# Rounds of four HGRN heads and of two mLSTM heads: loops on the engines, or the same rounds written out

## What is computed

```python
mod = silu(c) @ ada_w + ada_b                       # 2048 x 12288: shifts, scales, gates
h = rms_norm(x) * (1.0 + sc1) + sh1
proj = h @ w_in                                     # 2048 x 18448
hq, hf, hi, hg, mq, mk, mv, mi, mf, mo, ga, gb = split(proj)
o_hg, S_new = hgrn2_chunked(q, kk, logf, vv, S0)    # 16 heads of 128 x 128
y_a = head_rms_norm(o_hg, hg_norm_w) * silu(hg)
h_ml, C_new, n_new, m_new = mlstm_chunked(...)      # 8 heads of 128 x 256
y_b = head_rms_norm(h_ml, ml_norm_w) * sigmoid(mo)
merged = sigmoid(ga) * y_a + sigmoid(gb) * y_b
x = x + g1 * (merged @ w_out)
h = rms_norm(x) * (1.0 + sc2) + sh2
up = h @ w_up                                       # then a convolution of width 3 and gelu
x = x + g2 * (y @ w_down)
y = rms_norm(x, final_norm_w)                       # outputs: y, and all the new states
```

## Time and profile before

| | us |
|---|---|
| median of 3 runs | 2377.02 |
| the 3 runs | 2376.34, 2377.02, 2384.3 |
| profiled execution: time | 2376.97 |
| profiled execution: span | 2375.2 |
| PE busy / weight loads (beside PE) | 2281.6 (96%) / 2091.9 (88%) |
| DVE / ACT / POOL busy | 1094.4 / 1011.7 / 325.4 |
| mean granted TensorE clock | 0.976 of full speed |

### The profile page before, as it was taken

One profiled execution on the slowest core, in us unless ns is written; L12 is line 12 of the kernel. 1 busy time (PEld: TensorE's weight loads), 2 busy tenths in 40 slices (PEclk: granted clock), 3 DMA queues, 4 the chain that ended last, 5 costly groups with the idle time before them and its releaser, 6 DMA issues.

```text
span 2375.2 us, 44862 instructions
## 1 busy us (share of the span) xinstructions
PE 2281.6 (96%) x17440; PEld 2091.9 (88%) x17440; DVE 1094.4 (46%) x1433; ACT 1011.7 (43%) x1370; POOL 325.4 (14%) x452
## 2 busy tenths in 40 slices
PE   6799999999999999999999996999999999999997
PEld 2299998899898899888889886999999999999996
DVE  0245445455464444344343555454555555544443
ACT  2445544453454335343444435444444443433332
POOL 2000111211221212111211223000000000010000
PEclk8799999999999999999999997999999999999998
DMA  9966665566665566576566463666656555655552
GB/s 327 378 186 214 188 200 173 183 203 197 188 188 180 179 217 212 189 223 214 176 206 204 156 222 116 209 198 194 195 186 192 187 162 162 206 162 164 165 169 76
DMA packets 406627, 460.11 MB, mean 194 GB/s; under 512 B 14699, under 2 KB 379811, under 8 KB 405265
## 3 DMA queue, kind: packets, MB, share of 16 engines
q1 hardware_dynamic: 394401, 409.54, 54.8%
q0 software_dynamic: 11744, 46.03, 5.8%
q10 hardware_dynamic: 336, 2.36, 0.3%
HBM read 431.48 MB, written 26.39 MB: 193 GB/s over the span
## 4 chain that ended last, share of the span: by engine, by line
PE 91%; issue 3%; DMA 3%; ACT 1%; DVE 1%; POOL 1%; SPq 0%; POOLq 0%; ACTq 0%; DVEq 0%
PE ps L547 27%; PE ps L549 25%; PE ps L548 25%; PE ab L558 3%; DMA uraw<-in_ada_w 2%; PE R L526 2%; PE R L720 1%; PE ps L623 1%; PE R L747 1%; PE ab L565 0%; PE R L701 0%; PE R L732 0%; PE R L832 0%; PE R L825 0%; ACT whi L931 0%
## 5 line engine op out<-in xcount | busy, mean ns | idle before, releaser
L547 PE MATMUL ps<-xh,whi 128*128 128x288 f32 x3968 | 1205.0, 304 | 30.5 <-issue 21.5
L1293 DVE TENSOR_TENSOR wlo<-raw,whi 128x1024 fp32r<-128x1024 f32 x584 | 735.1, 1262 | 1028.3 <-ACT whi L931 1027.2
L549 PE MATMUL ps<-xh,wlo 128*128 128x288 f32 x3968 | 1176.2, 296 | 0.8 <-issue 0.8
L548 PE MATMUL ps<-xl,whi 128*128 128x288 f32 x3968 | 1176.2, 296 | 0.0
L931 ACT ACTIVATE whi<-raw 128x1024 fp32r<-128x1024 f32 x584 | 615.9, 1057 | 885.1 <-PE ps L549 790.3
L547 PEld LDWEIGHTS ps<-xh,whi 128*128 128x128 f32 x3968 | 751.0, 189 | 109.0 <-issue 97.8
L548 PEld LDWEIGHTS ps<-xl,whi 128*128 128x128 f32 x3968 | 751.7, 189 | 0.0
L549 PEld LDWEIGHTS ps<-xh,wlo 128*128 128x128 f32 x3968 | 750.6, 189 | 0.0
L547 PE MATMUL ps<-ffh,whi 128*128 128x288 f32 x704 | 209.5, 298 | 0.0
L549 PE MATMUL ps<-ffh,wlo 128*128 128x288 f32 x704 | 207.5, 295 | 0.0
L548 PE MATMUL ps<-ffl,whi 128*128 128x288 f32 x704 | 207.2, 294 | 0.0
(11 more groups left out here) (355 smaller groups left out, 1587.6 us busy)
## 6 DMA issues: line engine op xcount, KB each, us to landing
raw<-in_w_in SPq DMA_DIRECT2D x288, 512.0 KB, 5.0
raw<-in_w_up SPq DMA_DIRECT2D x176, 512.0 KB, 3.6
araw<-in_ada_w SPq DMA_DIRECT2D x96, 512.0 KB, 3.9
raw<-in_w_down SPq DMA_DIRECT2D x88, 512.0 KB, 3.6
uraw<-in_ada_w SPq DMA_DIRECT2D x64, 512.0 KB, 8.5
raw<-in_w_out SPq DMA_DIRECT2D x32, 512.0 KB, 3.6
araw_up<-in_ada_w SPq DMA_DIRECT2D x32, 512.0 KB, 4.3
S<-in_state_hgrn POOLq DMA_DIRECT2D x16, 512.0 KB, 5.1
```

The source lines that it names most:

```text
L547: mm(o, whi[:, s, kk, cols], hi[:, kt0 + kk, :], start=first and kk == 0, stop=False)
L548: mm(o, whi[:, s, kk, cols], lo[:, kt0 + kk, :], start=False, stop=False)
L549: x = mm(o, wlo[:, s, kk, cols], hi[:, kt0 + kk, :], start=False, stop=last and kk == KC - 1)
L1293: TT(wlo[:, s], raw[:, s], whi[:, s].bitcast(F32), ALU.subtract).then_inc(lo_done, 1)
```

## The change

Each of the loops over HGRN rounds and mLSTM rounds becomes a Python loop, so that its body stands three times (on SP seven times in all) in the program, with constants where registers were. The order of matmuls, activations, vector operations and DMAs is the same, and so are all conditions of waits. The loops over w_up and w_down rounds stay. The diff, cut to its core:

```diff
@@ sync
             hg_stage(0, first=True)
-            with sp.Fori(1, 4) as i:
+            for i in range(1, 4):
                 hg_stage(i)
-            with sp.Fori(0, 4) as i:
+            for i in range(0, 4):
                 ml_stage(i)
@@ tensor
-            with pe.Fori(0, 3) as i:
+            for i in range(0, 3):
                 stream(hg_base(i + 1), HG_KINDS, A_HG + 3 + 3 * i, turns(in_order(HG_TURNS, HG_DUE_PE), hg_step, 4 * i, i))
             stream(ml_base(0), ML_KINDS, A_ML, turns(in_order(HG_TURNS_ML, HG_DUE_PE), hg_step, 12, 3))
             pe.wait_ge(hg["out"], HH + FREE)
-            with pe.Fori(0, 3) as i:
+            for i in range(0, 3):
                 stream(ml_base(i + 1), ML_KINDS, A_ML + 3 + 3 * i, turns(in_order(ML_TURNS, ML_DUE_PE), ml_step, 2 * i, i))
@@ scalar (the loop over HGRN rounds, and in the same way the one over mLSTM rounds)
-            with act.Fori(0, 3) as i:
+            for i in range(0, 3):
                 def hook(q):
                     hg_prologue(q, i)
@@ vector (both loops in the same way)
-            with dve.Fori(0, 3) as i:
+            for i in range(0, 3):
                 def hook(q):
@@ gpsimd
-            with pool.Fori(0, 3) as i:
+            for i in range(0, 3):
                 hg_heads(i, 4 * i, i + 1)
...
-            with pool.Fori(0, 3) as i:
+            for i in range(0, 3):
                 ml_heads(i, 2 * i)
```

## The result

| | kernel before | changed kernel |
|---|---|---|
| median of 6 runs | 2376.89 us (2373.08 to 2384.3) | 2364.26 us (2360.16 to 2369.8) |
| ratio | | 0.9939, 95% interval 0.9922 to 0.9955 |
| profiled execution | 2376.97, span 2375.2 | 2369.21, span 2367.2 |

By the ratio the changed kernel is faster by 0.61%; on 2376.9 us that is 14.5 us, with an interval from 10.7 to 18.5. The two medians differ by 12.6 us. Forecast were 10.9 us and 2366.1; the time lies in the stated range. A second set of runs, beside the experiments, gave 0.9947 (0.9928 to 0.9967), with medians 10.8 us apart.

What follows compares the result with a forecast made beforehand. PE was taken to bound the kernel, its idle time coming from loop jumps. Waits of 8.41, short waits of 0.8 and clock of 1.7 summed to 10.9 us, giving 2366.1 us, in a range from 2361.0 to 2371.0.

Steps and rivals of the forecast that it cites:

- What bounds, and where: Whole kernel: PE bounds, busy 2281.6 of 2375.2 us; its idle time in looped rounds comes from jumps back over long bodies.
- The four waits and the two short ones: PE at HGRN and mLSTM loop jumps, and inside chunks: four waits go for 8.41 us, two short ones for 0.8.
- The clock: PE behind the first HGRN jump's wait: 3.40 us at half clock goes, gain 1.7 us, 0 or 3.4 in another execution.
- more goes: Rival, chance 0.17: half-clock dips near 785 and 1313.76 us go too, 4.8 us more, giving 2361.3 us.
- What stays: PE's waits behind mLSTM round 3 (3.23 us) and in mLSTM round 0 for `WQ` (2.4) and `Kt` (1.0) stay.
- the register work of the other engines: SP, ACT, DVE and POOL in the loops: some hundred register operations go, on engines that wait for PE; worth 0.
- The new closeness: Start of HGRN rounds 2 and 3: without the table load, PE reaches `tr` 0.8 us after POOL's `WQ` copy, so hidden.
- The sum: Whole kernel: 8.41 + 0.8 + 1.7 = 10.9 us gained, giving 2366.1 us; chance 0.60.
- The case that the jump is not the cause, or costs only a branch's price: Rival at PE's four jumps, chance 0.04: writing the rounds out gains only 4 x 0.21 = 0.8 us, giving 2376.2 us.
- the slower one: Rival, chance 0.04: PE's straight code runs dry in looped rounds, 2.98 us a place; eight places give 2389.9 us.

Runs made afterwards that it cites:

- the second profile: Kernel before and changed kernel, both profiled once more unaltered; seven stages took 1044.92 and 1032.66 us, the changed kernel's ratio in that set was 0.9947.
- the old hooks: HG_TURNS_ML 1, 8, 16, 23, as in the changed kernel; one run on it used 2, 9, 16, 23 instead and measured a ratio of 0.9918.

## Why the prediction was right, and where it was off

**What bounds, and where: right.** PE's idle time in the looped rounds was the whole matter, and it was its own jumps. The branch rows carried that: 5.1 and 3.5 us where the body is long, 0.21 where it is short. The experiment with three w_up rounds in a turn moved this price into a stage that had none, and with two rounds in a turn it stayed away.

**The four waits and the two short ones: right in kind, under-sized.** All six went. But 8.41 + 0.8 = 9.2 us is the idle time that the profile prints, and a wait costs more than that. HGRN round 3 has no half clock in either kernel, and lost 167.26 - 164.07 = 3.19 us for a printed 2.93; in the second profile 167.48 - 164.07 = 3.41 for 3.15. Each time 0.26 us more. The timeline shows it: a matmul's printed time is 0.29 us, but the next starts 0.13 behind it, so the last one hides 0.16 us of a stop; and the first one behind a stop stands 0.39 and is followed after 0.23, which is 0.10 more. Six waits make 1.5 us, if each of the short ones costs as much. The mLSTM jumps without a short wait bear it out: with PE's HGRN loop alone written out, 1.14 and 1.66 us printed, 1.37 and 1.90 lost. With one it is roughly so: mLSTM round 2 has 1.21 + 0.26 us printed in two waits, and 134.21 - 132.33 = 1.88 lost.

**The clock: nearly right.** 1.7 us were forecast. HGRN round 2 lost 168.84 - 164.07 = 4.77 us, of which 2.98 + 0.26 are the wait, so 1.5 are the clock; 4.62 and 1.5 in the second profile. Half the clock still follows the wait behind mLSTM round 3 (0.56 over 6.8 us). In mLSTM round 0 it stood behind the wait for `Kt` before and now stands behind the one for `WQ`, so it moved and did not go, and the case "more goes" did not come. In the changed kernel:

```profile
768.70:772.20 3.50, 3.50 (x17) 3.50 (x18) 1.02 (x1) 3.46 (x4) 3.39 (x5) 0.57 0.00 0
```

**What stays: right for the data wait, a little off in mLSTM round 0.** The wait behind mLSTM round 3 is 3.23 us in both. The one for `WQ` fell from 2.4 to 2.0 us and that for `Kt` from 1.0 to 0.5. The second is not shown to be of the change's making: it was 0.14 us with PE's HGRN loop alone written out and 1.29 with both of PE's. Of the first, the profiles say this much: POOL starts its copy 0.44 us after ACT's copies end in the kernel before, and 0.12 us after in the changed one.

```profile
764.21 2.85 ACT L1107 ACTIVATE WQ<-SQ 128x1536 f32<-128x1536 f32 x2
```

```profile
767.18 1.46 POOL L1780 COPY WQ<-SQ 128x1536 f32<-128x1536 f32 x1 [15.70 <-ACT WQ L1107]
```

ACT's copies end at 767.06 here, at 769.96 in the kernel before with POOL at 770.40. The wait is 2.36 us in all four profiles where POOL's loop is kept and 2.04 in all six with the old hooks where it isn't, with PE's loops or without. So the 0 that I took for the register work of the other engines was 0.3 us at this place, where PE waits for POOL; that the code ahead of it on POOL is the cause is argued, not shown. mLSTM round 0 gained 0.9 and 1.2 us, as much as the two waits lost. HGRN round 1 gained 0.25: PE's wait ahead of its first matmul is 0.74 to 0.75 us where PE's HGRN loop is kept and 0.44 to 0.45 where it is written out, whatever the other engines have. That is PE's own register work or the entry into its loop, which I had put at nothing.

**The new closeness: right, and its condition shown.** I put POOL's copy 0.8 us ahead of PE's `tr` because the table load goes. In the changed kernel it ends at 439.05 + 1.47 = 440.52 and PE starts at 441.55:

```profile
439.05 1.47 POOL L1780 COPY WQ<-SQ 128x1536 f32<-128x1536 f32 x1 [15.71 <-ACT WQ L1107]
```

```profile
441.55 0.49 PE L526 MATMUL R<-ident,WQ 128*128 128x128 f32 x3
```

With the table load kept (PE's loops alone) 0.8 - 1.28 = -0.5 should be left, and PE waited 0.45 us. The margin measured with everything written out is 1.03 us, a little more, because POOL starts its copy 0.12 us behind ACT's there and 0.28 where its loop is kept. So the 0.7 us a round that the other engines' loops cost once PE no longer stops is mostly the table load, and 0.16 of it POOL's later start; the table load alone was not tried.

**The sum.** 9.2 in printed waits, 1.5 that the profile doesn't print, 1.5 of clock, 0.9 in mLSTM round 0, 0.25 in HGRN round 1: 13.4, against 13.2 by stages and 10.9 forecast. The term that was mis-sized is the first: I took the idle time of a row for the time lost, 9.2 us for what cost 10.7. The second pair of profiles says the same: 8.9 printed in five waits, 1.3 that isn't, 1.5 of clock, 1.2 in mLSTM round 0 and 0.2 in HGRN round 1, less 0.7 for the new wait for `mV`, make 12.4, against 12.3 by stages. Of the 0.9 us, 0.6 is the wait for `Kt`, which varies by itself. The case that the jump is not the cause, or costs only a branch's price, is out, and so is the slower one. The Trainium skill, "Advanced Engine Details and Errata", section "Control Flow Timing", has about 108 ns for a compare-and-branch; the traces have 0.21 us for a short turn and 3.4 to 5.3 for a long one.

## What to carry to other kernels

Before a loop on TensorE is judged harmless, look at its compare-and-branch by source line: bodies of up to 1,724 instructions (matmuls, weight loads and control instructions counted, as the trace records them) jumped back in 0.2 us here, one of 2,585 took 5 us, of which the queue hid 2, and a turn that is short enough does the same as writing out. Take the count from the trace and not from the program's rows: the program gave 402 matmuls for a round of which the trace records 420. Write out the other engines with it where a compiler puts something at the head of their bodies (a table load), because TensorE's stop no longer covers it. Read a stop of TensorE as its printed idle time plus about a quarter of a microsecond, plus about 1.5 us where the granted clock is at half for 3.4 us behind it.

## What the runs showed of the hardware

- TensorE's compare-and-branch: 76 to 83 ns when it falls through, 0.21 to 0.24 us when it jumps back over 863 or 1,724 instructions, 3.4 to 3.9 over 2,064, 5.0 to 5.3 over 2,585 and 2,829. On ACT, DVE, POOL and SP it took at most 67 ns in these loops.
- The half clock behind a stop of about 3 us is not a matter of the stop's length alone: 2.82 us had it, 3.15 in the same run had not, and this repeated in three profiles. Nor does it take 3 us: with everything but PE written out two stops of 1.67 and 1.63 us, 5.7 us apart, were followed by 7.0 us at 0.53, and two of 1.63 us, as far apart, in the round before were not.
- Loops over long bodies on PE fetched more than the same rounds written out, 119 packets of instructions against 110; loops over short bodies fetched less, 110 against 137.
